# Attention scores of two heads on the two 64-row halves of TensorE, and output sums in two PSUM banks

## What is computed

```python
# "diff": differential attention, 8 pairs of heads, head size 64
sc = einsum('bqhcd,bshcd->bhcqs', q, k) * scale      # c = 0, 1: the two heads of a pair
p  = softmax(sc);  a = p[:, :, 0] - lam * p[:, :, 1]
o  = einsum('bhqs,bshe->bqhe', a, v)                 # v has 128 columns a pair
o  = rmsnorm(o, subln_g) * (1 - lam_init)
# "na": neighborhood attention, 16 heads of size 64, a window of columns and a position bias
p  = softmax(q . k * scale + bias);  o = p . v
# "b2": second block, 8 heads causal ("moba") and 8 heads causal with a forget term ("fox")
s  = q . k * scale (+ c[t] - c[s] for fox), masked where key > query;  o = softmax(s) . v
```

## Time and profile before

| what | value |
|---|---|
| timed runs | 1448.38 us median of 3 (1447.18 to 1448.45) |
| span of the profiled execution | 1445.4 us from its first to its last instruction |
| PE busy | 1424.5 us, 99% of the span, 6864 matmuls |
| VectorE, ScalarE, GpSimd busy | 870.8 us, 747.6 us, 88.8 us |
| chain that ended last, by engine | PE 92%, DVE 4%, issue 2%, ACT 1%, POOL 1% |
| chain that ended last, by line | L271, L272, L273 26% each; L759 2%, L795 2%, L784 1% |

### The profile page before, as it was taken

One profiled execution on the slowest core, in us unless ns is written; L12 is line 12 of the kernel. 1 busy time (PEld: TensorE's weight loads), 2 busy tenths in 40 slices (PEclk: granted clock), 3 DMA queues, 4 the chain that ended last, 5 costly groups with the idle time before them and its releaser, 6 DMA issues.

```text
span 1445.4 us, 20776 instructions
## 1 busy us (share of the span) xinstructions
PE 1424.5 (99%) x6864; PEld 1185.4 (82%) x6864; DVE 870.8 (60%) x1113; ACT 747.6 (52%) x1216; POOL 88.8 (6%) x101
## 2 busy tenths in 40 slices
PE   9999999999999999999999999999999999999999
PEld 7888888778888888888878988888888898888887
DVE  5555575766555565555685665555657756566654
ACT  6444464656444454444535654444545465465553
POOL 2100110010000000000250000000013000000000
PEclk9999999999999999999999999999999999999999
DMA  9877746325555646556453145556575513555551
GB/s 304 243 224 217 219 159 204 117 67 162 191 185 189 202 154 202 187 180 203 163 182 118 45 142 193 189 189 201 178 209 168 175 59 101 175 166 184 182 184 54
DMA packets 189938, 248.21 MB, mean 172 GB/s; under 512 B 15194, under 2 KB 128101, under 8 KB 189760
## 3 DMA queue, kind: packets, MB, share of 16 engines
q1 hardware_dynamic: 187904, 241.35, 52.6%
q0 software_dynamic: 1984, 6.21, 1.8%
HBM read 246.33 MB, written 1.17 MB: 171 GB/s over the span
## 4 chain that ended last, share of the span: by engine, by line
PE 92%; DVE 4%; issue 2%; ACT 1%; POOL 1%; DMA 0%; SPq 0%; ACTq 0%; DVEq 0%
PE ps L271 26%; PE ps L273 26%; PE ps L272 26%; PE ps L759 2%; PE ps L795 2%; PE ps L554 1%; PE ps L784 1%; DVE wlo L264 1%; PE ps L284 1%; DVE h L475 1%; PE ps L366 1%; PE ps L961 1%; PE ps L285 1%; PE ps L289 1%; PE ps L331 1%
## 5 line engine op out<-in xcount | busy, mean ns | idle before, releaser
L264 DVE TENSOR_TENSOR wlo<-raw,whi 128x1024 fp32r<-128x1024 f32 x450 | 561.8, 1258 | 384.6 <-ACT whi L256 384.5
L256 ACT CAST whi<-raw 128x1024 fp32r<-128x1024 f32 x450 | 470.0, 1051 | 366.6 <-PE ps L273 350.0
L271 PE MATMUL ps<-whi,xhi 128*128 128x512 f32 x1280 | 500.7, 391 | 3.3 <-DVE wlo L264 3.3
L272 PE MATMUL ps<-wlo,xhi 128*128 128x512 f32 x1280 | 498.7, 390 | 0.0
L273 PE MATMUL ps<-whi,xlo 128*128 128x512 f32 x1280 | 498.6, 390 | 0.0
L271 PEld LDWEIGHTS ps<-whi,xhi 128*128 128x128 f32 x1280 | 240.6, 188 | 53.2 <-DVE wlo L264 3.8
L273 PEld LDWEIGHTS ps<-whi,xlo 128*128 128x128 f32 x1280 | 240.7, 188 | 50.3
L272 PEld LDWEIGHTS ps<-wlo,xhi 128*128 128x128 f32 x1280 | 240.8, 188 | 49.6
L271 PE MATMUL ps<-whi,thi 128*128 128x512 f32 x400 | 160.5, 401 | 0.0
L273 PE MATMUL ps<-whi,tlo 128*128 128x512 f32 x400 | 156.5, 391 | 0.0
L272 PE MATMUL ps<-wlo,thi 128*128 128x512 f32 x400 | 156.0, 390 | 0.0
(11 more groups left out here) (181 smaller groups left out, 1139.2 us busy)
## 6 DMA issues: line engine op xcount, KB each, us to landing
raw<-in_ffn_wg_dram SPq DMA_DIRECT2D x176, 256.0 KB, 2.9
raw<-in_ffn_wu_dram SPq DMA_DIRECT2D x176, 256.0 KB, 3.0
raw<-in_ffn_wd_dram SPq DMA_DIRECT2D x176, 256.0 KB, 3.0
raw<-in_w_ffn_up_dram SPq DMA_DIRECT2D x88, 256.0 KB, 3.5
raw<-in_w_in_dram SPq DMA_DIRECT2D x80, 256.0 KB, 3.2
raw<-in_diff_w_in_dram SPq DMA_DIRECT2D x48, 256.0 KB, 3.0
raw<-in_na_w_in_dram SPq DMA_DIRECT2D x48, 256.0 KB, 3.2
raw<-in_w_ffn_down_dram SPq DMA_DIRECT2D x44, 256.0 KB, 3.1
```

Source lines behind the costliest of these rows:

```text
L256: nc.scalar.copy(whi[:, s], raw[:, s]).then_inc(s_hi, 1)
L264: nc.vector.tensor_tensor(wlo[:, s], raw[:, s], whi[:, s].bitcast(F32), ALU.subtract).then_inc(s_lo, 1)
L271: nc.tensor.matmul(outs[t], ahi[:, c], whi[:, s, i], start=start, stop=False)
L272: nc.tensor.matmul(outs[t], ahi[:, c], wlo[:, s, i], start=False, stop=False)
```

## The change

- Scores: head c of a pair is computed from partitions 64c to 64c + 63 of `qT` and of one K tile `kT`, that is with 64-row matmuls, into a bank of its own. Task i uses the banks Z and Z + 1 (even i) or Y + 2 and Y + 3 (odd i). The fp32 matmuls of both heads now stand together, and in b2 the fp32r terms of both follow.
- `kT1`, its zeros and `zero_pool` are gone; ScalarE writes head 1's half of K into `kT`.
- Output sums: groups 0 and 2 use bank Y, groups 1 and 3 use Y + 1. `pv(8)` and `pv(12)` wait until VectorE has scaled groups 0 and 1.

```diff
-        kT1 = osb[:].rearrange("p t (k s) -> p (t k) s", s=S)
...
-        def zero_pool(pool, m, r):
-
-            pool.wait_ge(s_rx, r + 1)
-            nc.gpsimd.memset(kT[HD:P], 0.0).then_inc(s_kz, 1)
-            pool.wait_ge(s_kz, 2 * m + 1)
-            nc.gpsimd.memset(kT1[0:HD], 0.0).then_inc(s_kz, 1)
-            pool.wait_ge(s_kz, 2 * m + 2)
...
-                nc.scalar.copy(kT1[HD:P, 2 * bk:2 * bk + 2, :].rearrange("p k c -> p (k c)"),
+                nc.scalar.copy(kT[HD:P, 2 * bk:2 * bk + 2, :].rearrange("p k c -> p (k c)"),
                                ps[HD:P, Y + bk]).then_inc(s_kta, 1)
...
+        def score_banks(i):
+
+            return Z if i % 2 == 0 else Y + 2
+
+        ATTN_SRC = [4, 20, 32]
+
...
-            pe.wait_ge(s_kz, 2 * (m + 1))
...
                 w = keys(kind, t) * P
                 for c in range(2):
-                    o = ps[:, Z + i % 2, c * S:c * S + w]
+                    o = ps[:, score_banks(i) + c, 0:w]
+                    half = slice(c * HD, (c + 1) * HD)
+                    ins = nc.tensor.matmul(o, qT[half, p, t * P:(t + 1) * P], kT[half, p, 0:w], start=True,
+                                           stop=not (kind == "b2" and p >= 4))
+                for c in range(2):
+                    o = ps[:, score_banks(i) + c, 0:w]
                     fox = kind == "b2" and p >= 4
-                    ins = nc.tensor.matmul(o, qT[:, p, t * P:(t + 1) * P], (kT, kT1)[c][:, p, 0:w], start=True, stop=not fox)
                     if fox:
                         pe.wait_ge(s_fr, (p - 4) // 2 + 1)
 
                         ins = nc.tensor.matmul(o, cL[:, t * P:(t + 1) * P], cR[:, 2 * (p - 4) + c, 0:w], start=False, stop=True)
                     if kind == "b2":
-                        ins = nc.tensor.matmul(ps[:, Z + i % 2, c * S + t * P:c * S + (t + 1) * P], identr, causr,
+                        ins = nc.tensor.matmul(ps[:, score_banks(i) + c, t * P:(t + 1) * P], identr, causr,
                                                start=False, stop=True, skip_group_check=True)
                 ins.then_inc(s_sc, 1)
...
             def pv(i):
                 p, t = TASKS[i]
                 pe.wait_ge(s_ate, b + i + 1)
+                if t == 1 and p % 4 == 0:
+                    pe.wait_ge(s_src, ATTN_SRC[m] + p // 4 + 1)
...
-                        ins = nc.tensor.matmul(ps[:, Y + 2 * t + p // 4, (p % 4) * P + c * w:(p % 4) * P + (c + 1) * w],
+                        ins = nc.tensor.matmul(ps[:, Y + p // 4, (p % 4) * P + c * w:(p % 4) * P + (c + 1) * w],
```

More of the change, by code:

```diff
@@ L180, in build @@
         s_kta = sem("kT1_ready")
-        s_kz = sem("kT_rest_zero")
         s_sc = sem("scores_done")
@@ L818, in squares @@
                     ins = nc.scalar.activation(sqa[:, (g % 2) * 512 + hd * P:(g % 2) * 512 + (hd + 1) * P],
-                                               ps[:, Y + g, hd * P:(hd + 1) * P], ACT.Square,
+                                               ps[:, Y + g % 2, hd * P:(hd + 1) * P], ACT.Square,
                                                accum_out=sso[:, g // 2, 4 * (g % 2) + hd:4 * (g % 2) + hd + 1])
@@ L840, in attn_act @@
                         act.wait_ge(s_at, b + i - 2)
-                    src = ex[:, i % NEX] if kind == "na" else ps[:, Z + i % 2].rearrange("p (c k) -> p c k", c=2)
+                    src = ex[:, i % NEX] if kind == "na" else ps[:, score_banks(i):score_banks(i) + 2]
                     for c in range(2):
@@ L880, in scaled @@
                 nc.vector.tensor_tensor(o_sb[:, g // 2, (g % 2) * 512:(g % 2 + 1) * 512].rearrange("p (g c) -> p g c", g=n),
-                                        ps[:, Y + g].rearrange("p (g c) -> p g c", g=n),
+                                        ps[:, Y + g % 2].rearrange("p (g c) -> p g c", g=n),
                                         by.unsqueeze(2).broadcast_to([P, n, 512 // n]), ALU.mult).then_inc(s_src, 1)
@@ L895, in attn_dve @@
                     dve.wait_ge(s_sc, b + i + 1)
-                    sc = ps[:, Z + i % 2].rearrange("p (c k) -> p c k", c=2)[:, :, 0:w]
+                    sc = ps[:, score_banks(i):score_banks(i) + 2, 0:w]
                     if kind == "na":
@@ L1136, in _ @@
             pre_pool(pool, steps, 1)
-            zero_pool(pool, 0, 1)
             for g in range(4):
@@ L1147, in _ @@
             pre_pool(pool, steps, 4)
-            zero_pool(pool, 1, 4)
             pool.wait_ge(s_nab, 16 * GR * GR)
@@ L1159, in _ @@
             pre_pool(pool, steps, 6)
-            zero_pool(pool, 2, 6)
             nc.gpsimd.memset(lf4, 0.0).then_inc(s_one, 1)
```

## The result

The changed kernel takes 1454.81 us (median of 7 runs, 1451.59 to 1468.92) against 1448.08 (7 runs, 1447.04 to 1448.58) beside it. The medians are 6.7 us apart, a ratio of 1.0046; the ratio over all runs, which two runs above 1468 us raise, is 1.0074 (95% interval 1.0049 to 1.0099). Forecast were 1455.8 us. The total is close, but most terms under it are not, and the spread is new: the kernel before stays within 1.6 us here, this one spreads over 17.

What follows compares the result with a forecast made beforehand. TensorE was taken to bound the kernel, with 92% of the chain of waits; 1.5 (na) + 2.3 (b2) + 0.8 (diff scores) + 2.8 (diff waits) = +7.4 us on 1448.4 gave 1455.8 us, range 1443 to 1462 (some 0.85).

Steps and rivals of the forecast that it cites:

- The overlap: Scores: one pass of four saved by running heads side by side, 0.21 us per 256-key task, nothing with 128 keys.
- price of a switch: Scores: each change between 128-row and 64-row matmuls costs 0.16 us, 0.32 us a task.
- The rival of everything side by side: Scores: both passes and weight loads of the two heads run side by side; 1436.4 us, chance 0.04.
- the rival of overlap alone: Scores: heads overlap and changing between half and full rows does not empty the array; 1444.3 us, chance 0.27.
- na: Neighbourhood attention: 14 tasks on the path, each 0.11 us slower, +1.5 us.
- b2: Second block's attention: eight 256-key tasks at +0.11 us, seven 128-key tasks at +0.32, less 0.8 for matmul order; +2.3 us.
- The 0.8 us for the order: Second block's attention: grouping both heads' fp32 passes ahead of the fp32r ones saves 0.05 us in 15 tasks.
- The waits in diff: Differential attention: pv(8) and pv(12) wait for VectorE's scaling of the shared output banks, +1.6 and +1.2 us, sum +2.8.
- The zeroing: GpSimd ahead of the neighbourhood attention: removing six zeroing instructions costs or gives nothing.
- The clock: TensorE: the forecast would be wrong if its granted clock, 1.00 before, fell with half the rows idle; no size given.

Runs made afterwards that it cites:

- e8: As e5, but both heads' scores computed from rows 0 to 63, so nothing can overlap; one run of 1452.31 us.
- e5: Kernel before with the whole change in the neighbourhood attention (na) alone, zeroing kept; 1445.2 us against 1447.27, ratio 0.9985.
- e6: As e5, with the same change also in the second block's attention (b2); 1445.35 us, ratio 0.9983.
- e12: As e1, but TensorE does eight idle matmuls ahead of pv(8) and pv(12) in the differential attention (diff); 1450.87 us, ratio 1.0022.
- e1: Kernel before with only the two output banks and their waits added, scores as before; 1453.22 us against 1447.34, ratio 1.0040.
- e2: Kernel before with GpSimd's zeroing moved behind the bias sum of the neighbourhood attention; 1452.38 us, ratio 1.0036.
- e7: The changed kernel once more, on the same chip as e5, e6 and e8; 1473.0 us (4 runs), ratio 1.0156.
- e4: The changed kernel with GpSimd's zeroing kept, its only difference; 1449.29 us, ratio 1.0016.
- e11: As e5, with GpSimd's bias sum in 16 instructions in place of two; 1440.0 us, ratio 0.9952.
- e13: The changed kernel with GpSimd's bias sum in 16 instructions in place of two; 1445.76 us, ratio 0.9994.

## Why the prediction was right and wrong

The direction and the total were right, the total by luck: terms that were off in both directions made it up.

- **The overlap** is the step that failed: "As matmuls start in order, only head 0's second pass and head 1's first can run together: at best one pass of four is saved, 0.21 us a task." It is two of four, 0.43 us (e8 against e5, single records of the changed kernel). With my own price of a switch, this alone turns 29 x 0.11 = +3.2 us into 29 x -0.11 = -3.2.
- **The price of a switch** was right in kind and size: 0.14 to 0.15 us in na against 0.16. Both halves showed where the prediction said they would, ahead of the scores and in the transposes behind them. The rival of everything side by side had the overlap right and left this out; the rival of overlap alone had neither. na comes out 2.2 us shorter instead of 1.5 longer.
- **b2** was +2.3 forecast and is +0.1 at the full clock (e6). With the overlap put right the sum of the prediction gives 8 x -0.11 + 7 x 0.32 - 0.8 = +0.6; the rest is that both kinds of task change by less than its terms say (256 keys -0.07 to -0.09 us, 128 keys with the forget term +0.11). The 0.8 us for the order was not tested by itself.
- **The waits in diff** were right: both places, the engine they wait for, and +2.7 measured (e12) against 2.8. In e1 each then costs another 1.2 us in clock (e1 against e12), which the forecast didn't have.
- **The zeroing** is the second step that failed: "What stood behind them, the bias sum of na, starts at 721.69 and takes 19.60 us, done 44 us before its user." True, and the wrong question. The sum slows VectorE, for which PE waits 6.8 us in place of 3.3. e2, which moves nothing else, makes the stretch 3.5 us longer; about 2.5 of the 4.2 us ahead of na are this wait and the rest is clock.
- **The clock** was named as what could make me wrong ("if the clock granted to PE [...] fell with half the rows idle"), with no price. It fell in b2, which adds 17.0 us in the profiled run and 23.1 in e7's, and nothing in e4 and e6. The median run has a clock of 0.994 against 0.995 to 0.996 in the three shortest, so some of the 2.4 us from 1452.4 to 1454.81 is clock as well; where it fell in that run is not on record.

With the right sizes for overlap, switch, waits and zeroing, and the clock whole in b2, one gets about 1452. The clock, which had no price in the forecast, brought the median nearer to it.

## What to carry to other kernels

Two 64-row fp32 matmuls on the two halves saved two of their four passes here, but each turn between 64-row and 128-row work cost about 0.15 us in na. That paid for 256 columns and not for 128. By these prices it should pay more if the packed matmuls of several tasks stood together, since they would share the turns; that is an estimate, not run. Before an idle instruction on GpSimd is removed, look at what moves up behind it and which VectorE instructions it then runs beside. Chopping the long one gave about 5 us (e11 against e5), more than the 2.1 that the new scores give in na. A new wait of 2 us on TensorE can cost more than itself: look at the clock granted behind it.

## What the runs showed of the hardware

- fp32 matmuls on different row halves start 6 ns apart, pass for pass, and their weight loads 7 ns apart.
- A switch between 64-row and 128-row matmuls costs 0.14 to 0.15 us in na's stream.
- GpSimd additions of 9.0 to 10.0 us with two inputs in SBUF stretched the VectorE operation beside each of them from 1.2 us to 8.48, 9.36, 9.91 and 10.04 us. With the sum in 16 pieces of 1.3 to 2.3 us, the longest was 2.11 us in e11 and 2.32 in e13.
- In e1 two TensorE waits of 2.15 and 1.95 us were each followed by 3.4 us at half the clock, and with matmuls in the waits (e12) by none. Behind the same wait of 3.3 us ahead of na, half the clock lasted nothing, 3.4 or 6.8 us in e6, e5 and e8, which are the same up to there.
- In b2 the same stream of work, 6.08 us busy in 7.00, was followed by 54.6 us at half the clock in e7 and by none in e4, e6 and e13; 5.88 us busy in 7.00, of 128-row work, was followed by none in the kernel before.
